# Half-column level products, centring folded into a transpose, and a re-ordered output norm in a 512-step RWKV-7 scan

## The reference, cut to what matters

```python
def step(state, inp):                      # rwkv7_scan
    r_t, w_t, k_t, v_t, kk_t, a_t = inp
    sa = jnp.einsum('bhvk,bhk->bhv', state, -kk_t)
    state = (state * w_t[:, :, None, :] + sa[..., None] * (kk_t * a_t)[:, :, None, :]
             + v_t[..., None] * k_t[:, :, None, :])
    return state, jnp.einsum('bhvk,bhk->bhv', state, r_t)
...
def group_norm(o, gn_w, gn_b):             # per head, GN_EPS = 64e-5
    mu = jnp.mean(o, axis=-1, keepdims=True)
    var = jnp.mean(jnp.square(o - mu), axis=-1, keepdims=True)
    y = (o - mu) * lax.rsqrt(var + GN_EPS)
    nB, S, H, N = o.shape
    return y.reshape(nB, S, H * N) * gn_w.astype(F32) + gn_b.astype(F32)
...
for d in range(2):                         # rwkv7_mixer
    w_log = -jax.nn.softplus(-(w0[d] + jnp.tanh(xw @ w1[d]) @ w2[d])) - 0.5
    decay = jnp.exp(-jnp.exp(w_log.astype(F32)))
    a = jax.nn.sigmoid(a0[d] + (xa @ a1[d]) @ a2[d])
    g = jax.nn.sigmoid(xg @ g1[d]) @ g2[d]
    kd = heads(k * (1 + (a - 1) * k_a))
    ...
    bonus = jnp.sum(rh * kd * r_k.astype(F32), axis=-1, keepdims=True) * vh
    dir_out.append((group_norm(o, gn_w, gn_b) + bonus.reshape(nB, S, D)) * g.astype(F32))
```

## Time and profile before

| | us |
|---|---|
| median of 3 runs | 2702.97 (2702.12 to 2707.06) |
| the profiled execution, whole | 2702.67 |
| its span, first to last instruction | 2700.9 |
| TensorE busy | 2503.9 (93%) |
| VectorE busy | 1309.4 (48%) |
| ScalarE busy | 867.2 (32%) |
| GpSimd busy | 763.7 (28%) |
| the eight pairs, about 928 to 1619 us of the span | 691 |

### The profile page before, as it was taken

One profiled execution on the slowest core, in us unless ns is written; L12 is line 12 of the kernel. 1 busy time (PEld: TensorE's weight loads), 2 busy tenths in 40 slices (PEclk: granted clock), 3 DMA queues, 4 the chain that ended last, 5 costly groups with the idle time before them and its releaser, 6 DMA issues.

```text
span 2700.9 us, 53426 instructions
## 1 busy us (share of the span) xinstructions
PE 2503.9 (93%) x22468; PEld 1784.3 (66%) x22468; DVE 1309.4 (48%) x1989; ACT 867.2 (32%) x1442; POOL 763.7 (28%) x431
## 2 busy tenths in 40 slices
PE   7999899999799998988898899899998899998998
PEld 5876578887344577867777783588876666763443
DVE  6055330130634756566656652549421699836011
ACT  4266332332223333322322221346422322243011
POOL 3301244444000333232423320244443233330101
PEclk9999999999899998988999999899999999999999
DMA  4321122322122000000000011124322233322222
GB/s 145 98 66 60 59 86 86 102 87 92 53 78 70 30 9 9 3 9 9 9 4 9 3 34 48 61 91 188 126 86 86 87 116 117 94 86 70 78 66 74
DMA packets 49915, 181.30 MB, mean 67 GB/s; under 512 B 5600, under 2 KB 5856, under 8 KB 49440
## 3 DMA queue, kind: packets, MB, share of 16 engines
q1 hardware_dynamic: 46064, 166.98, 19.0%
q10 hardware_dynamic: 3632, 11.08, 1.0%
HBM read 167.49 MB, written 10.55 MB: 66 GB/s over the span
## 4 chain that ended last, share of the span: by engine, by line
PE 81%; issue 10%; DVE 6%; ACT 2%; POOL 1%; DMA 0%; DVEq 0%; POOLq 0%; ACTq 0%
PE ps L561 14%; PE ps L558 13%; PE ps L559 13%; PE ps L560 13%; PE ps L782 10%; PE ps L601 2%; PE ps L791 2%; PE ps L735 1%; PE ps L1014 1%; PE ps L648 1%; POOL ring_lo L2046 1%; PE ps L924 1%; PE ps L663 1%; PE ps L638 1%; DVE arena L1834 1%
## 5 line engine op out<-in xcount | busy, mean ns | idle before, releaser
L2046 POOL TENSOR_TENSOR ring_lo<-ring,ring_hi 128x1024 fp32r<-128x1024 f32 x198 | 481.3, 2439 | 908.4 <-ACT ring_hi L1065 908.4
L561 PE MATMUL ps<-arena,ring 128*128 128x512 f32 x1024 | 454.1, 601 | 26.1 <-DVE arena L1756 11.7
L560 PE MATMUL ps<-u_lo,ring_hi 128*128 128x512 f32 x968 | 385.4, 398 | 0.0
L561 PEld LDWEIGHTS ps<-arena,ring 128*128 128x128 f32 x1024 | 195.4, 192 | 280.1 <-issue 239.4
L1065 ACT ACTIVATE ring_hi<-ring 128x1024 fp32r<-128x1024 f32 x198 | 207.3, 1051 | 75.5 <-DMA ring<-in_wall 72.2
L558 PE MATMUL ps<-mlp_u_hi,ring_hi 128*128 128x512 f32 x512 | 212.3, 415 | 8.8 <-POOL ring_lo L2046 7.4
L560 PEld LDWEIGHTS ps<-u_lo,ring_hi 128*128 128x128 f32 x968 | 184.1, 190 | 43.5
L558 PE MATMUL ps<-mid_hi,ring_hi 128*128 128x512 f32 x512 | 208.2, 407 | 0.0
L559 PE MATMUL ps<-mlp_u_hi,ring_lo 128*128 128x512 f32 x512 | 204.4, 399 | 0.0
L560 PE MATMUL ps<-mid_lo,ring_hi 128*128 128x512 f32 x512 | 202.5, 395 | 0.0
L559 PE MATMUL ps<-mid_hi,ring_lo 128*128 128x512 f32 x512 | 202.4, 395 | 0.0
(11 more groups left out here) (382 smaller groups left out, 4428.3 us busy)
## 6 DMA issues: line engine op xcount, KB each, us to landing
ring<-in_wall SPq DMA_DIRECT2D x273, 512.0 KB, 3.6
s_tables<-arena ACTq DMA_DIRECT2D x16, 512.0 KB, 3.2
arena<-s_tables SPq DMA_DIRECT2D x16, 512.0 KB, 3.6
arena<-bias_lines SPq DMA_DIRECT2D x16, 448.0 KB, 4.5
arena<-in_lora SPq DMA_DIRECT2D x8, 384.0 KB, 3.1
h<-in_x SPq DMA_DIRECT2D x1, 2048.0 KB, 7.4
out<-arena ACTq DMA_DIRECT2D x8, 256.0 KB, 2.8
consts<-in_consts SPq DMA_DIRECT2D x1, 1312.0 KB, 13.7
```

Source lines behind the costliest of these rows:

```text
L560: return nc.tensor.matmul(y, w_hi, low, start=False, stop=x == k - 1)
L561: return nc.tensor.matmul(y, ring[:, at:at + P], rhs(x), start=x == 0, stop=x == k - 1)
L2046: G.tensor_tensor(ring_lo[:, slot], ring[:, slot], ring_hi[:, slot].bitcast(F32), ALU.subtract).then_inc(sem("weights_split"), 1)
```

## The change

- Level products. `each` into banks B and C becomes `each_half`: of each 64 moving columns only the 32 that the level alters are multiplied, read and written with a stride pattern (`columns_of_level`). VectorE's two additions run on the same 256 of 512 columns. The product for X stays whole.
- Centring. v is transposed by a matrix eye - 1/64 in place of eye, so the scan's output comes out centred. `out_means` and `out_centered` go. The squares are taken by ScalarE at the end of the pair, and the variance product sums (its 1/64 is in the activation's scale).
- 1/deviation. Sqrt on ScalarE and reciprocal on VectorE are replaced by two activations on ScalarE, Ln and then Exp with scale -0.5.
- Low-rank products. At levels 1 and 2 each direction uses only its own 64 rows of the stationary and moving tiles, and both directions are issued together, after the products of direction 0. The products for the gate (step 2) stay as they are.
- Order on VectorE. The features have six steps in place of four; scaling moves from level 4 to level 3, gating from level 5 to level 4, the bonus terms from j = 3, 4 to j = 0, 1, the last features from level 5 and j = 1 to j = 3, 4, 5. After the last pair the bonus is taken at once and the variances two products earlier.

```diff
+        def columns_of_level(a, l, h):
+
+            return a.rearrange("p (b h w) -> p b h w", h=2, w=1 << l)[:, :, h, :]
 
...
 
                 k = 2 * step + d
-                nc.tensor.matmul(bank(4 * d + b), lora2[:, k * P:(k + 1) * P],
-                                 [lo_w, lo_w, lo_a, lo_a, lo_g[0], lo_g[1]][k],
+                rows = slice(d * HEAD, (d + 1) * HEAD) if step < 2 else slice(0, P)
+                nc.tensor.matmul(bank(4 * d + b), lora2[rows, k * P:(k + 1) * P],
+                                 [lo_w, lo_w, lo_a, lo_a, lo_g[0], lo_g[1]][k][rows, :],
                                  start=True, stop=True).then_inc(sem("z_ready"), 1)
...
+                for c in range(NCH):
+                    for e in range(2):
+                        rows, at = slice(e * HEAD, (e + 1) * HEAD), slice(c * CH, (c + 1) * CH)
+                        mm = nc.tensor.matmul(columns_of_level(out[rows, at], l, h), a[rows, at],
+                                              columns_of_level(b[rows, at], l, h), start=True, stop=True)
+                return mm
+
             A, B, C, O = [[bank(4 * d + x) for d in range(2)] for x in range(4)]
 
-            def out_means(n):
+            def out_bonus(n, F):
...
                 for d in range(2):
                     pe.wait_ge(sem("o_copied"), n(2, d + 1))
-                    nc.tensor.matmul(O[d], const("head_mean"), o_sb[d], start=True, stop=True
-                                     ).then_inc(sem("mean_ready"), 1)
-
-            def out_bonus(n, F):
-
-                for d in range(2):
-                    pe.wait_ge(sem("o_centered"), n(2, d + 1))
                     pe.wait_ge(sem("bonus_terms"), n(2, d + 1))
                     nc.tensor.matmul(O[d], const("head_sum"), F[d]["kd"], start=True, stop=True
                                      ).then_inc(sem("bonus_ready"), 1)
...
                 for d in range(2):
                     pe.wait_ge(sem("bonus_done"), n(2, d + 1))
                     pe.wait_ge(sem("o_squared"), n(2, d + 1))
-                    nc.tensor.matmul(O[d], const("head_mean"), dev[d], start=True, stop=True
+                    nc.tensor.matmul(O[d], const("head_sum"), dev[d], start=True, stop=True
                                      ).then_inc(sem("var_ready"), 1)
 
             def pair(parity, n, prev, nxt):
                 F = feats[parity]
 
-                if prev:
-                    out_means(prev)
                 for d in range(2):
...
                         pe.wait_ge(sem("x_taken"), n(10, k + 1))
-                        each(B[d], R[d]["TT"], R[d]["X"]).then_inc(sem("dt_ready"), 1)
+                        each_half(B[d], R[d]["TT"], R[d]["X"], l, 1 - d).then_inc(sem("dt_ready"), 1)
                         if l < LEVELS - 1:
-                            each(C[d], R[d]["X"], R[d]["TT"]).then_inc(sem("dtt_ready"), 1)
-                        if nxt and l <= 2:
-                            if l == 1 and d == 0:
+                            each_half(C[d], R[d]["X"], R[d]["TT"], l, d).then_inc(sem("dtt_ready"), 1)
+                        if nxt and l <= 2 and d == 0:
+                            if l == 1:
                                 pe.wait_ge(sem("lora2_landed"), nxt(16, 16))
-                            hidden_product(nxt, l - 1, d, 0)
+                            pe.wait_ge(sem("x_taken"), n(10, k + 2))
+                            pe.nop(nofuse=True)
+                            for other in range(2):
+                                hidden_product(nxt, l - 1, other, 0)
                         if l == 3:
                             if prev:
                                 pe.wait_ge(sem("deviation"), prev(2, d + 1))
@@ -879,7 +888,7 @@
                             each_turned(A[d], F[d]["ka"]).then_inc(sem("scores_ready"), 1)
                         if l == 4 and d == 0:
                             pe.wait_ge(sem("v_staged"), n(1, 1))
-                            each_turned(A[0], v_st).then_inc(sem("scores_ready"), 1)
+                            each_turned(A[0], v_st, "center").then_inc(sem("scores_ready"), 1)
...
-            out_means(last)
+            out_bonus(last, feats[(DT - 1) % 2])
 
             def last_outputs(x):
 
                 if x == 2:
-                    out_bonus(last, feats[(DT - 1) % 2])
-                elif x == 4:
                     out_variances(last)
...
-            def out_squares(n):
-                for d in range(2):
-                    act.wait_ge(sem("o_centered"), n(2, d + 1))
-                    nc.scalar.activation(dev[d], o_sb[d], ACT.Square).then_inc(sem("o_squared"), 1)
-
             def out_deviations(n):
                 for d in range(2):
                     act.wait_ge(sem("var_ready"), n(2, d + 1))
-                    nc.scalar.activation(dev[d], bank(4 * d + 3), ACT.Sqrt, bias=const("eps", 1, 1)
+                    nc.scalar.activation(dev[d], bank(4 * d + 3), ACT.Ln, scale=1.0 / HEAD, bias=const("eps", 1, 1)
                                          ).then_inc(sem("deviation"), 1)
+                for d in range(2):
+                    act.wait_ge(sem("deviation"), n(2, d + 1))
+                    nc.scalar.activation(dev[d], dev[d], ACT.Exp, scale=-0.5).then_inc(sem("deviation_inverse"), 1)
 
...
                     act.wait_ge(sem("scores_ready"), n(15, 3 + d))
                     taken(R[d]["L"], bank(4 * d + 1), "l_copied")
-                if prev:
-                    out_squares(prev)
                 for d in range(2):
                     act.wait_ge(sem("scores_ready"), n(15, 9 + d))
                     taken(F[d]["be"], bank(4 * d + 2), "turned")
@@ -1408,9 +1411,11 @@
                 for d in range(2):
                     act.wait_ge(sem("o_ready_rw"), n(16, 15 + d))
                     taken(o_sb[d], bank(4 * d + 3), "o_copied")
+                for d in range(2):
+                    act.wait_ge(sem("o_copied"), n(2, d + 1))
+                    nc.scalar.activation(dev[d], o_sb[d], ACT.Square).then_inc(sem("o_squared"), 1)
 
...
-                if step == 0:
-                    for d in range(2):
-                        r = F[d]
+                for d in range(2):
+                    r = F[d]
+                    if step == 0:
                         dve.wait_ge(sem("z_taken"), n(6, 1 + d))
                         src, dst = (r["al"], r["ro"]) if d == 0 else (r["al"][:, ::-1], r["ro"][:, ::-1])
                         V_.tensor_tensor_scan(dst, const("carry", 0, SEQ), src, 0.0, ALU.mult, ALU.add
                                               ).then_inc(sem("decay_scanned"), 1)
-                    for d in range(2):
-                        r = F[d]
+                    elif step == 1:
                         dve.wait_ge(sem("decay_scanned"), n(2, d + 1))
                         TT(r["al"], r["ro"], r["al"], ALU.subtract).then_inc(sem("decay_summed"), 1)
-                    return
-                if step == 1:
-                    for d in range(2):
-                        r = F[d]
+                    elif step == 2:
                         dve.wait_ge(sem("z_taken"), n(6, 3 + d))
                         TS(r["kd"], r["be"], pair_col("k_a", n), der[:, bass.ds(n(1, OMKA), 1)], ALU.mult, ALU.add
                            ).then_inc(sem("kd_factor"), 1)
-                    return
-                d = step - 2
-                r = F[d]
-                dve.wait_ge(sem("decays_ready"), n(6, 3 * (d + 1)))
-                V_.tensor_copy(ends_at[d], ends(r["ro"], d)).then_inc(sem("p_end_ready"), 1)
-                STT(out=r["al"], in0=r["al"], scalar=-1.0, in1=pair_tile(kk, n), op0=ALU.mult, op1=ALU.mult
-                    ).then_inc(sem("al_ready"), 1)
-                dve.wait_ge(sem("p_end_ready"), n(2, d + 1))
-                TT(r["ro"], r["ro"], pair_tile(rT, n), ALU.mult).then_inc(sem("features_v"), 1)
-
-            def out_centered(n):
-                for d in range(2):
-                    dve.wait_ge(sem("mean_ready"), n(2, d + 1))
-                    TT(o_sb[d], o_sb[d], bank(4 * d + 3), ALU.subtract).then_inc(sem("o_centered"), 1)
+                    elif step == 3:
+                        dve.wait_ge(sem("decays_ready"), n(6, 3 * (d + 1)))
...
                 for d in range(2):
                     dve.wait_ge(sem("bonus_ready"), n(2, d + 1))
@@ -1847,37 +1839,31 @@
                 for d in range(2):
                     dve.wait_ge(sem("scores_ready"), n(15, 1 + d))
                     TT(chunks(R[d]["T"]), chunks(bank(4 * d)), mask("level_n", d), ALU.mult).then_inc(sem("n_masked"), 1)
-                if prev:
-                    out_centered(prev)
                 for d in range(2):
                     dve.wait_ge(sem("l_copied"), n(2, d + 1))
                     TT(chunks(R[d]["TT"]), chunks(bank(4 * d + 1)), mask("level", d * LEVELS), ALU.mult
                        ).then_inc(sem("tt_masked"), 1)
-                masked(5, 1, "Ma", 2, "strict")
                 if prev:
```

(35 more changed lines are left out.)

21 lines of the change are left out of this document (13 added, 8 removed).

## The result

The changed kernel takes 2627.8 us (median of 4 runs, 2624.7 to 2630.3) against 2702.6 (2699.4 to 2707.1) for the kernel before, measured beside it: a ratio of 0.9722, interval 0.9704 to 0.9739, a gain of 74.8 us. The forecast was 2643 with a range of 2596 to 2682, a gain of 59.7. The profiled execution took 2630.3, its span is 2628.5: 72.4 us less than the span before.

What follows compares the result with a forecast made beforehand. The prediction took TensorE to bound the kernel, as the chain for 81% of the span. Gains summing to 59.5 us, taken from the profiled 2702.7, gave 2643 us, with a range of 2596 to 2682.

Steps and rivals of the forecast that it cites:

- the chunk steps: VectorE's new order in the chunk steps: 7.5 us gained, 5.2 given back a pair, 13.8 net over six pairs.
- The first wait: First chunk step's wait, with gating moved earlier: falls from 4.0 to about 0.3 us, 3.7 gained a pair.
- the one for u: Chunk steps: TensorE's 3.0 us wait for VectorE's copy of u goes, with the features at level 5.
- Half columns: Level products on half the moving columns: each costs 0.95 of a whole one, 4.4 us over eight pairs.
- the half price: Level products: a half-column product would cost 0.47 us instead of 0.93 if streaming alone set the pace.
- the rival at 2595: Streaming binds: half-column level products cost half, 48 us more gain than forecast; chance 18%.
- Head means: Mean instructions leave the scores of pairs 1 to 7, 13.4 us; waits ahead of five pairs go, 3.0 us.
- Low-rank products: Both directions run beside each other, 1.06 us instead of 2.12: 7.0 us at level 1, 2.9 at level 2.
- Level 2 and level 4 waits, table loads: ScalarE: two loads and about 3.3 us TensorE idle before level 3; no load at decays, 7.5 us gained at level 4.
- End of the pairs: The point in the trace where the eight pairs finish, expected near 1567.
- After pair 7: Next layer's last tile, which waited 5.88 us: chain loses 1.9, 3.4 and 5.4, so 7.5 us gained.
- The granted clock: TensorE's clock in the pairs, left at 0.93; 3 us more or less at half clock a pair is 12 us.

Runs made afterwards that it cites:

- Experiment 3: Changed kernel with VectorE's order of before: 2652.7 us; with only the gating back at level 5: 2642.0; with bonus terms at j = 2 and 6: 2611.5.
- experiment 1: Changed kernel with TensorE's level products on whole columns again, VectorE still adding half: 2626.0 us, ratio 0.9725.
- experiment 5: Changed kernel with the low-rank products of levels 1 and 2 on all 128 rows again: 2635.6 us, ratio 0.975.
- Experiment 4: Changed kernel with Ln and Exp issued at level 3: 2604.1 us; with Square replacing Ln: 2613.9; with the old Sqrt and reciprocals: 2629.4.

## Why the prediction was right, and where it was not

Sign and range held; the 59.5 us came out as 72.4 of span. That it is not further off is partly luck, for errors of opposite sign stood in the sum: the steps brought 19.9 us more than forecast, the end 1.4 more, scores and levels 8.6 less.

- *The term that was mis-sized: the chunk steps.* Forecast 13.8 us for pairs 1 to 6 and nothing in pair 0; measured 31.4 and 2.4 (and nothing in pair 7). Of a pair the forecast had 7.5 gained and 5.2 given back. What was given back shows in the starts of pair 2's steps, here those of j = 1, 2, 3, 5 and 6:

```profile
1137.10 0.57 PE L911 MATMUL ps<-arena,u 64*64 64x64 f32 x8
...
1141.20 0.57 PE L911 MATMUL ps<-arena,u 64*64 64x64 f32 x8
...
1144.92 0.56 PE L911 MATMUL ps<-arena,u 64*64 64x64 f32 x8
...
1149.84 0.56 PE L911 MATMUL ps<-arena,u 64*64 64x64 f32 x8
...
1152.63 0.56 PE L911 MATMUL ps<-arena,u 64*64 64x64 f32 x8
```

j = 3 and 4 take 2.46 us each; j = 1 takes 4.10 and j = 2 3.72, so 1.64 and 1.26 more, where the forecast had 2.3 and 1.7. j = 5 takes 2.79 and j = 6 2.78, behind the features of j = 4 and 5: 0.3 each, where it had 0.6, and no wait is listed for them. In all 3.6 given back, not 5.2. At j = 0 I took 1.2 for the decayed state's surplus, 1.75 for the bonus terms and 0.7 of slack. The rows give 1.24 - 0.41 = 0.83 of surplus (0.41 is the same pair of operations later in the steps), 1.75, and 1.64 lost, so 0.94 of slack; at j = 1, (1.89 - 0.41) + 0.74 - 1.26 = 0.96. So surplus and slack were both mis-sized, 0.37 us too much and 0.24 too little. Experiment 3 bears out the mechanism: 2.7 us a pair come back once the bonus terms leave j = 0 and 1. The other half of the miss is on the gained side: 5.4 net and 3.6 given back make 9.0 gained in pair 2, not 7.5. The first wait gave 3.7 and the one for u 3.0, as forecast; 2.3 are left for the features at j = 1, forecast at 0.8, and for the granted clock of these steps, 1.00 after and 0.88 before; the windows of the two kernels:

```profile
1134.60:1157.50 22.90, 19.73 (x481) 1.00 0.08 21
```

```profile
1152.30:1180.50 28.20, 20.64 (x481) 0.88 0.07 17
```

- *Half columns: 4.4 us forecast, none measured* (experiment 1: ratios 0.9725 and 0.9722). Starts are 29.1 ns apart with 32 moving columns and 29.3 with 64. I was right to refuse the half price, and the rival at 2595 fell; I took 27.5 ns from the difference of two weight loads, which is below the 29 that a load of 64 columns sets. Those two loads differ in rows as well as columns, so they could not show by themselves that the columns alone count.
- *Head means: 13.4 + 3.0 forecast.* The scores of pair 2 lost 1.73 us, not 1.92, and the 0.61 ahead of them went. Over pairs 1 to 7 scores and waits ahead of them came to 16.6 us less, about the forecast, though in pairs 3 and 5 a part of it is a shorter slow stretch.
- *Low-rank products: 9.9 us forecast, 7.8 measured* by experiment 5, of which its rows show 6.2; level 1 came to 7.19 instead of 6.95, level 2 to 12.02 instead of 11.85.
- *Level 2 and level 4 waits, table loads.* Two loads of 1.28, an idle time of 3.14 (forecast about 3.3), no load at the decays, 0.85 of idle at level 4 (about 1.0): each as written. But the forecast credited the new form of 1/deviation with 7.5 us at level 4 and saw its price only as gain not taken at level 2. Experiment 4 puts both sides together: old form and new form tie (2629.4 and 2627.8).
- *End of the pairs: near 1567 forecast, 1555.6 measured.* Of the 63.2 us up to there, 29.6 lie in scores and levels (38.2 forecast with the half columns), of which 1.0 in pair 0, and 33.7 in the steps.
- *After pair 7: 7.5 forecast, 8.9 measured* (the distance from the end of the steps to the first product with u in the next layer, 1649.66 before and 1577.51 after, falls from 30.8 to 21.9; the sum took 7.5 although its three terms add to 10.7). Besides the wait of 5.88 and the means, a slow stretch went that I had not counted: behind that wait the clock stood at 0.51 from 1642.76 to 1646.20, which is 1.7 us of products at twice their length; after, it is 1.00 throughout. On the chain, from the first activation of 1/deviation to the scaling, 7.2 us became 3.5, 3.7 less and not 5.4, although one of the two loads cost nothing: Ln's table load did not wait for its operand, standing at 1557.71, with ScalarE then idle for 3.54 us until its input came. I had both loads on the path.

The granted clock, 0.93 over the pairs in the earlier trace rows and 0.95 after, was the open end I named ("3 us more or less a pair is 12 us on the sum"), and it went the good way: 58 us at 1.2 GHz instead of 92. All 34 us of that lie in the steps, where TensorE waits anyway for part of the time, so it is worth less than half of them; an estimate from pair 2, the 2.3 above less 0.8 for the features, is 1.5 a pair, some 9 us.

## What to carry to other kernels

Look for waits that cost twice: once as idle time, and again in the products behind them that run at half clock; here Ln and Exp, issued a level later, earned 14 us of idle time and up to 12 of clock. Before shrinking a product, find out which of its two sizes sets the pace: where loading and streaming cost the same, halving one is worth nothing. And when an operation moves to another queue, count what it stands ahead of: a form that is cheaper by itself (1/deviation) tied with the old one until it was issued behind the copies that TensorE waits for, and then gave 24 us.

## What the runs showed of the hardware that I had not expected

- Starts of small float32 products on alternating row halves: 29.3 ns for 64 weight and 64 moving columns, 29.1 for 64 and 32, 28.0 for 32 and 64, 15.9 for 32 and 32 inside a group (23.9 over the whole block with its two breaks). Strided moving columns: 29.2, no cost.
- The granted clock fell to 1.2 GHz in a block of products with 8 moving columns although TensorE was never idle in it, and stayed full through blocks with 32 and 64.
- A table load can run ahead of its activation's wait: 1557.71, with 3.54 us of idle behind it.
- Two VectorE operations of 1.21 us together (1150.16 to 1151.37) hold up the next copy for TensorE by 0.33 us, and the list of waits shows nothing of it; the starts do.
